# Moving a 4 MB memory-to-memory copy of a window state from the first projection to behind the samples' first seven page loads

## Chip, cores and metric

One core of one Trainium2 chip runs the whole program in one launch. The metric is device time in microseconds (us) of that core, the median of several executions. Lower is better.

## What is computed

The program is one inference step of a two-layer decoder. A prompt of 512 tokens and 8 samples of 8 new tokens each go through the same weights. Layer 0 mixes differential attention (4 heads) and sparse attention (4 query heads, with compressed, selected and window branches), layer 1 is gated linear attention, and each is followed by a squared-ReLU MLP (1024 to 4096 to 1024). Each sub-layer's input is scaled and shifted by a modulation computed from a conditioning vector (`silu(c) @ ada_w + ada_b`).

One of the fourteen outputs matters here. The window branch keeps, for every sample, the last 256 rows of keys and values. The new state drops the oldest 8 rows and appends the 8 new ones:

```python
win_all = jnp.concatenate([win_buf, jnp.stack([kw, vw], axis=2)], axis=1)   # win_buf: (8, 256, 2, 2, 128) f32
...
return y, (ka, va, cmp_new, sel_new, win_all[:, S:])                        # S = 8
```

So 248 of the 256 rows per sample are plain copies of an input: 8 x 248 x 512 x 4 bytes, 3968 KB, moved from device memory to device memory without passing through any engine's arithmetic. No computation of the step reads the copied output.

## The kernel before

The tensor engine (PE) carries the work, in this order: turning the inputs, the samples' compression (L980), the **first projection** (L1082 to L1084), the prompt's compression (L1131), the **prompt's attention** (`p_scores`, `p_turn`, `p_values`, L1168 to L1213), the **samples' attention** (`s_keys` to `s_back`, L1250 to L1301), the output projection, the MLP of layer 0, layer 1, and the second MLP. ScalarE (ACT) and VectorE (DVE) evacuate its results and split weights into high and low parts.

**The first projection** goes over 7 blocks of 512 columns (queries, keys, values, and so on, `pj_units`, L501), each over 5 tiles of tokens (four of 128 prompt tokens, one of the 64 sample tokens). A tile is 8 steps of three matmuls of 512 columns. Between the tiles PE does one unit of the modulation: `ada_late(0, u - 1)` (L946), which folds the last unit (L935), waits for the 1 MB of `ada_w` that this unit needs (L952), and multiplies it (L927, 32 small matmuls).

**SP's queue** is an order written out by hand (L649 to L789). For this stage it alternates `load_late(0, i)` (L686, 1 MB each into one of two places, waiting at L690 until PE has multiplied the unit before the last one) with `load_in(j)` (L712, two weights of 1 MB for a projection block). So a load of `ada_w` is requested when PE has ended a unit, and needed two units later.

**POOL's queue** (L791 to L899) loads 16 cached pages for the compression (L804), zeroes two scratch tiles (L809, L810), requests the copy of the state (L812), then stores each finished tile of keys and values (L834 to L849), and then requests the pages for the samples' attention, in a loop over 16 half steps `v` (L856). Even `v`: two pages of keys and two of values (L867); odd `v`: two pages of the selected branch (L871) and one load of the window state (L873). There are 8 places (`KV_PLACES`) in the weight ring for them. The place of `v == 7` holds something of the prompt's attention, so POOL waits there for its end (`o_kept`, L861). Later half steps wait until PE has used a place (L863). At the program's end POOL waits for everything that it sent, the copy included (L899).

Of the kernel before, what the change touches and what calls it, by code (L numbers as in the profile page):

```python
# [35 lines left out]
NS, DS = 8, 8  # L36
# [3 lines left out]
PAST, PAGE = 256, 128  # L40
# [76 lines left out]
def decoder_program(nc, a, out, const_cols):  # L117

    ctx = ExitStack()
    with ctx, nc.allow_non_contiguous_dma(reason="small vectors, gate columns"):  # L120
# [3 lines left out]
        def sem(name):  # L124
            return ctx.enter_context(nc.semaphore(name))
# [251 lines left out]
        out_stored = sem("out_stored")  # L377
# [415 lines left out]
        def _(pool):  # L793
# [15 lines left out]
            pool.memset(qAs[:, :, :, :], 0.0).then_inc(scratch_zero, 1)  # L809
            pool.memset(qBs[:, :, :, :], 0.0).then_inc(scratch_zero, 1)  # L810

            pool.dma_start(out[12][0][:, 0:PAST - DS], a["state_win_kv"][0][:, DS:PAST]).then_inc(out_stored, 16)  # L812

            def kv_out(o_p, o_s, t):

                if t < NT:
                    return o_p[t * P:(t + 1) * P]
                return o_s
# [37 lines left out]
            for v in range(2 * NS):  # L856
                n = v // 2
                if v == 4:
                    pool.wait_ge(cmp_mm, 3)
                if v == KV_PLACES - 1:  # L860
                    pool.wait_ge(o_kept, HA + HB)  # L861
                if v >= KV_PLACES:
                    pool.wait_ge(spv_mm, v - KV_PLACES + 1)  # L863
                if v % 2 == 0:
                    for b, cache in enumerate((ck, cv)):
                        for pg in range(NPAGE):
                            pool.dma_start(kvb[v % KV_PLACES][:, 2 * b + pg, :], cache[bass.ds(page[n * NPAGE + pg], 1)].rearrange("o t c -> (o t) c")  # L867
                                           ).then_inc(kv_loaded[v % KV_PLACES // 2], 16)
                else:
                    for pg in range(NPAGE):  # L870
                        pool.dma_start(kvb[v % KV_PLACES][:, pg, :], cs[bass.ds(page[n * NPAGE + pg], 1)].rearrange("o t c -> (o t) c")  # L871
                                       ).then_inc(kv_loaded[v % KV_PLACES // 2], 16)
                    pool.dma_start(kvb[v % KV_PLACES][:, 2:4, :], win[n]).then_inc(kv_loaded[v % KV_PLACES // 2], 16)  # L873
# [29 lines left out]
        def _(pe):  # L903
# [164 lines left out]
            def token_tile(banks, tiles, base, split=None, gate=False):  # L1068

                for k in range(KC):  # L1070
                    if split is not None:
                        pe.wait_ge(h_split, split + k + 2)
                    _, w_hi, w_lo = unit(base + k // 4, 4)
                    for bank, (u, t) in zip(banks, tiles):
                        x_hi, x_lo = h_high_x(k, t), h_low(k, t)
                        if gate:
                            at = ps[:, 7, 32 * t:32 * t + 24]
                            pe.matmul(at, x_hi, gwin_r[:, k, :], start=k == 0, stop=False)
                            mm = pe.matmul(at[:, 0:12], x_lo, gwin_r[:, k, 0:12], start=False, stop=k == KC - 1)
                            if t == NT and k == KC - 1:  # L1080
                                mm.then_inc(gate_mm, 1)
                        pe.matmul(bank, x_hi, w_hi[:, k % 4, :], start=k == 0, stop=False)  # L1082
                        pe.matmul(bank, x_hi, w_lo[:, k % 4, :], start=False, stop=False)  # L1083
                        mm = pe.matmul(bank, x_lo, w_hi[:, k % 4, :], start=False, stop=k == KC - 1)  # L1084
                        if k == KC - 1:
                            mm.then_inc(gin_mm if u is None else pj_mm, 1)
# [254 lines left out]
            def out_projection(layer):  # L1341
# [5 lines left out]
                def products(m, k, parts):  # L1347

                    _, w_hi, w_lo = unit(base + m // 2)
                    hi, lo = w_hi[:, k, m % 2 * P:(m % 2 + 1) * P], w_lo[:, k, m % 2 * P:(m % 2 + 1) * P]  # L1350
                    first, last = k == come[0], k == come[-1]
                    for i in parts:
                        bank = ps[:, 2 * (m % 4) + i, 0:HALF]
                        pe.matmul(bank, hi, h_hi[:, k, halves[i]], start=first, stop=False)  # L1354
                        pe.matmul(bank, hi, hT_r[:, k, halves[i]], start=False, stop=False)  # L1355
                    for i in parts:
                        mm = pe.matmul(ps[:, 2 * (m % 4) + i, 0:HALF], lo, h_hi[:, k, halves[i]], start=False, stop=last)  # L1357
                    if last:
                        mm.then_inc(out_mm, 1)
# [35 lines left out]
            def mlp(layer):  # L1395
# [4 lines left out]
                def half_products(g, k, half):  # L1400

                    _, w_hi, w_lo = unit(g // 2)
                    hi, lo = w_hi[:, k, g % 2 * P:(g % 2 + 1) * P], w_lo[:, k, g % 2 * P:(g % 2 + 1) * P]
                    bank, cols = ps[:, 2 * g + half, 0:HALF], halves[half]
                    pe.matmul(bank, hi, h_hi[:, k, cols], start=k == 0, stop=False)
                    pe.matmul(bank, hi, hT_r[:, k, cols], start=False, stop=False)
                    mm = pe.matmul(bank, lo, h_hi[:, k, cols], start=False, stop=k == KC - 1)
                    if half and k == KC - 1:
                        mm.then_inc(up_mm, 1)
# [1519 lines left out]
```

## Time and profile before

| what | value |
|---|---|
| median of 3 runs | 1866.79 us (1862.47 to 1869.63) |
| the profiled execution, own time | 1866.58 us |
| its span, first to last instruction | 1864.9 us |
| PE busy | 96% of the span |
| DVE, ACT, POOL busy | 46%, 25%, 4% |
| mean granted clock of PE | 0.954 of full speed |
| mean DMA rate | 117 GB/s |

The page of the profile shows 40 slices of the span, 46.6 us each. The first projection lies in slices 2 to 7, the prompt's attention in 7 to 10, the samples' in 10 and 11. A granted clock of 1.00 is 2.4 GHz and one of 0.50 is 1.2 GHz. The chain of waits is followed back from the last instruction: what stands in it was, one after the other, what the end waited for.

### The profile page before, as it was taken

How to read it: one execution, taken by the hardware profiler on the slowest of the kernel's cores; microseconds unless marked ns; L12 is line 12 of the kernel's file. 1: busy time of each engine (PE TensorE's matmuls, PEld its weight loads, DVE VectorE, ACT ScalarE, POOL GpSimd, SP SyncE). 2: the span in 40 equal slices, each digit the busy share in tenths (PEclk: the TensorE clock that was granted, in tenths of full speed). 3: DMA queues.
4: the chain of work that ended last, by engine and by line, in shares of the span. 5: the costliest groups of instructions: out<-in, count | busy, mean ns of one | idle time of the engine just before them, and what ended most of it. 6: DMA issues, size and time to landing. Idle time of an engine off the chain costs nothing.

```text
span 1864.9 us, 32781 instructions
## 1 busy us (share of the span) xinstructions
PE 1782.5 (96%) x14208; PEld 1628.2 (87%) x14208; DVE 861.4 (46%) x1653; ACT 472.8 (25%) x774; POOL 78.4 (4%) x146
## 2 busy tenths in 40 slices
PE   6989999899889999999999899999989999999998
PEld 5868888678759999999999897788889999999997
DVE  4543333444344664545353623344465836444542
ACT  3412121234463321111111323122323211111112
POOL 2000001400120000000000000000000000000000
PEclk8999999989899999999999999888779999999998
DMA  9876664500171323222223455222133222222211
GB/s 350 287 251 231 208 204 128 218 1 1 48 236 36 91 91 91 68 90 90 69 89 127 149 172 174 86 71 94 52 119 91 83 76 90 84 73 90 90 46 51
DMA packets 160191, 219.02 MB, mean 117 GB/s; under 512 B 7271, under 2 KB 131198, under 8 KB 159630
## 3 DMA queue, kind: packets, MB, share of 16 engines
q1 hardware_dynamic: 148814, 177.52, 29.4%
q0 software_dynamic: 11264, 39.86, 6.0%
q8 instruction: 88, 1.44, 0.3%
q14 instruction: 25, 0.20, 0.0%
HBM read 199.66 MB, written 21.76 MB: 119 GB/s over the span
## 4 chain that ended last, share of the span: by engine, by line
PE 89%; DVE 5%; DMA 2%; issue 2%; ACT 1%; POOLq 0%; POOL 0%; ACTq 0%; DVEq 0%
PE ps L1451 14%; PE ps L1449 14%; PE ps L1448 13%; PE ps L1082 4%; PE ps L1084 4%; PE ps L1083 4%; PE ps L927 2%; PE ps L1194 2%; PE ps L1354 2%; DMA arena<-in_ada_w 2%; PE ps L1355 2%; PE ps L1357 2%; PE ps L1180 2%; PE ps L980 2%; PE ps L1209 1%
## 5 line engine op out<-in xcount | busy, mean ns | idle before, releaser
L1448 PE MATMUL ps<-arena_r,wring_r 128*128 128x288 f32 x1920 | 532.8, 292 | 0.0
L1451 PE MATMUL ps<-arena_r,wring_r 128*128 128x288 f32 x1920 | 411.3, 295 | 0.0
L1448 PEld LDWEIGHTS ps<-arena_r,wring_r 128*128 128x128 f32 x1920 | 360.5, 188 | 0.0
L1451 PEld LDWEIGHTS ps<-arena_r,wring_r 128*128 128x128 f32 x1920 | 307.0, 188 | 0.0
L1449 PE MATMUL ps<-arena_r,wring_r 128*128 128x288 f32 x1024 | 284.5, 294 | 0.0
L1922 ACT ACTIVATE wring_r<-wring 128x2048 fp32r<-128x2048 f32 x64 | 122.4, 1916 | 576.5 <-DMA wring<-in_mlp_w 576.5
L1449 PE MATMUL ps<-hbuf_r,wring_r 128*128 128x288 f32 x896 | 249.0, 294 | 0.0
L1449 PEld LDWEIGHTS ps<-arena_r,wring_r 128*128 128x128 f32 x1024 | 192.4, 188 | 0.0
L2664 DVE SCALAR_TENSOR_TENSOR xbuf<-ps,mod,xbuf 128x288 f32<-128x288 f32 (+1 forms) x128 | 56.1, 480 | 245.4 <-PE ps L1451 245.4
L1449 PEld LDWEIGHTS ps<-hbuf_r,wring_r 128*128 128x128 f32 x896 | 168.3, 188 | 0.0
L2636 DVE TENSOR_TENSOR wring_r<-wring,wring_r 128x2048 fp32r<-128x2048 f32 x64 | 146.2, 2285 | 6.1 <-ACT wring_r L1922 5.0
L1082 PE MATMUL ps<-wring_r,xbuf_r 128*128 128x512 f32 x360 | 149.0, 414 | 0.0
L1083 PE MATMUL ps<-wring_r,xbuf_r 128*128 128x512 f32 x360 | 141.2, 392 | 0.0
L1084 PE MATMUL ps<-wring_r,hbuf_r 128*128 128x512 f32 x360 | 141.0, 392 | 0.0
L2650 DVE TENSOR_SCALAR arena<-ps 128x576 f32<-128x576 f32 x64 | 48.4, 756 | 131.2 <-PE ps L1451 131.2
L2193 DVE TENSOR_TENSOR wring_r<-wring,wring_r 128x2048 fp32r<-128x2048 f32 x34 | 77.6, 2290 | 36.3 <-ACT wring_r L1717 35.4
L1082 PEld LDWEIGHTS ps<-wring_r,xbuf_r 128*128 128x128 f32 x360 | 68.2, 189 | 19.1 <-issue 6.1
L1354 PE MATMUL ps<-arena_r,wring_r 128*128 128x288 f32 x256 | 76.9, 306 | 4.3 <-DVE hbuf_r L2303 3.0
L1084 PEld LDWEIGHTS ps<-wring_r,hbuf_r 128*128 128x128 f32 x360 | 68.0, 189 | 14.9
L1083 PEld LDWEIGHTS ps<-wring_r,xbuf_r 128*128 128x128 f32 x360 | 68.3, 190 | 11.4
L1355 PE MATMUL ps<-hbuf_r,wring_r 128*128 128x288 f32 x256 | 75.5, 300 | 0.0
L1357 PE MATMUL ps<-arena_r,wring_r 128*128 128x288 f32 x256 | 68.3, 298 | 0.0
(395 smaller groups left out, 2755.1 us busy)
## 6 DMA issues: line engine op xcount, KB each, us to landing
wring<-in_mlp_w SPq DMA_DIRECT2D x64, 1024.0 KB, 5.7
arena<-in_ada_w SPq DMA_DIRECT2D x40, 1024.0 KB, 6.1
wring<-in_even_w_in SPq DMA_DIRECT2D x14, 1024.0 KB, 7.4
wring<-in_gla_w_in SPq DMA_DIRECT2D x12, 1024.0 KB, 5.6
wring<-in_ada_w SPq DMA_DIRECT2D x4, 2048.0 KB, 18.2
xbuf<-xspill SPq DMA_DIRECT2D x2, 2304.0 KB, 9.4
arena<-in_cache_cmp_kv POOLq DMA_DIRECT2D x16, 256.0 KB, 6.8
wring<-in_cache_diff_k POOLq DMA_DIRECT2D x16, 256.0 KB, 3.8
```

Of the source, the lines that this page charges most:

```text
L1082: pe.matmul(bank, x_hi, w_hi[:, k % 4, :], start=k == 0, stop=False)
L1083: pe.matmul(bank, x_hi, w_lo[:, k % 4, :], start=False, stop=False)
L1084: mm = pe.matmul(bank, x_lo, w_hi[:, k % 4, :], start=False, stop=k == KC - 1)
L1354: pe.matmul(bank, hi, h_hi[:, k, halves[i]], start=first, stop=False)
L1355: pe.matmul(bank, hi, hT_r[:, k, halves[i]], start=False, stop=False)
L1357: mm = pe.matmul(ps[:, 2 * (m % 4) + i, 0:HALF], lo, h_hi[:, k, halves[i]], start=False, stop=last)
L1448: pe.matmul(bank, hi, x_hi[:, k, cols], start=k == 0, stop=False)
L1449: pe.matmul(bank, hi, x_lo[:, k, cols], start=False, stop=False)
L1451: mm = pe.matmul(bank, lo, x_hi[:, k, cols], start=False, stop=k == KC - 1)
L1922: act.activation(high, raw, ACT.Copy).then_inc(w_high, 1)
L2193: dve.tensor_tensor(low, raw, high.bitcast(F32), ALU.subtract).then_inc(w_split, 1)
L2636: dve.tensor_tensor(low, raw, high.bitcast(F32), ALU.subtract).then_inc(w_split, 1)
```

## The change

The request of the copy is taken from its place ahead of the loop over projection tiles, and put into the loop over the samples' half steps, at `v == 7`, before the wait for the end of the prompt's attention. Nothing else is different.

```diff
@@ -809,8 +809,6 @@
             pool.memset(qAs[:, :, :, :], 0.0).then_inc(scratch_zero, 1)
             pool.memset(qBs[:, :, :, :], 0.0).then_inc(scratch_zero, 1)
 
-            pool.dma_start(out[12][0][:, 0:PAST - DS], a["state_win_kv"][0][:, DS:PAST]).then_inc(out_stored, 16)
-
             def kv_out(o_p, o_s, t):
 
                 if t < NT:
@@ -858,6 +856,7 @@
                 if v == 4:
                     pool.wait_ge(cmp_mm, 3)
                 if v == KV_PLACES - 1:
+                    pool.dma_start(out[12][0][:, 0:PAST - DS], a["state_win_kv"][0][:, DS:PAST]).then_inc(out_stored, 16)
                     pool.wait_ge(o_kept, HA + HB)
                 if v >= KV_PLACES:
                     pool.wait_ge(spv_mm, v - KV_PLACES + 1)
```

## Rows read from the trace of the kernel before

**Rows 1.** Page: busy time, and shares of the chain of waits

```profile
PE 1782.5 (96%) x14208; PEld 1628.2 (87%) x14208; DVE 861.4 (46%) x1653; ACT 472.8 (25%) x774; POOL 78.4 (4%) x146
PE 89%; DVE 5%; DMA 2%; issue 2%; ACT 1%; POOLq 0%; POOL 0%; ACTq 0%; DVEq 0%
```

**Rows 2.** Waits of PE, 100 to 335 us: total, times, longest

```profile
PE ps L927 <- DMA arena<-in_ada_w: 7.2, 1, 7.2
```

**Rows 3.** Chain of waits, 88 to 135 us: start, length, what

```profile
101.97 20.54 DMA arena<-in_ada_w
122.51 0.04 issue
122.56 1.90 PE ps L927 x32
124.46 0.73 PE ps L1082
125.18 0.43 PE ps L1083
125.61 0.42 PE ps L1084
...
131.37 0.99 PE ps L927 x32
```

**Rows 4.** Chain of waits, 142 to 156 us, the same work undisturbed

```profile
145.97 0.99 PE ps L927 x32
146.96 0.43 PE ps L1082
147.39 0.23 PE ps L1083
147.62 0.23 PE ps L1084
...
153.21 0.99 PE ps L927 x32
```

**Rows 5.** Timeline of PE around the gap: start, length, instruction, idle before

```profile
115.09 0.29 PE L935 MATMUL ps<-cf,arena 128*128 128x18 f32 x2
122.56 1.90 PE L927 MATMUL ps<-arena,scT 128*9 128x128 f32 x32 [7.18 <-DMA arena<-in_ada_w]
```

**Rows 6.** Stretches: us, PE, PEld, DVE, ACT, POOL busy, granted clock, DMA share, GB/s

```profile
120.00:124.00 4.00, 1.44 (x28) 1.10 (x32) 0.00 (x0) 0.00 (x0) 0.00 (x0) 0.50 0.91 291
140.00:300.00 160.00, 160.00 (x1247) 131.49 (x1246) 59.09 (x140) 39.46 (x76) 13.04 (x24) 1.00 0.59 195
```

**Rows 7.** Timeline of POOL's queue

```profile
96.00 0.62 POOL L812 DMA_DIRECT2D out<-in_state_win_kv  x1
133.88 0.57 POOL L834 DMA_DIRECT2D out<-arena  x1 [37.26 <-DVE arena L2344]
...
344.72 1.11 POOL L867 DMA_DIRECT2D wring<-in_cache_diff_k  x2
...
357.51 1.06 POOL L867 DMA_DIRECT2D wring<-in_cache_diff_v  x2
489.42 1.06 POOL L871 DMA_DIRECT2D wring<-in_cache_sel_kv  x2 [130.84 <-DVE hbuf L2431]
```

**Rows 8.** DMA, 102 to 120 us: packets, MB, share of 16 engines; copy's time to landing

```profile
q0 software_dynamic: 56, 3.05, 39.8%
q1 hardware_dynamic: 1348, 1.36, 24.4%
out<-in_state_win_kv POOLq DMA_DIRECT2D x1, 3968.0 KB, 24.1
```

**Rows 9.** DMA issues at 94.7, at 109.2 and at 161.5 us: time to landing

```profile
arena<-in_ada_w SPq DMA_DIRECT2D x1, 1024.0 KB, 5.0
arena<-in_ada_w SPq DMA_DIRECT2D x1, 1024.0 KB, 16.3
arena<-in_ada_w SPq DMA_DIRECT2D x1, 1024.0 KB, 9.4
```

**Rows 10.** DMA, 383 to 488 us: all its queues

```profile
q8 instruction: 5, 0.08, 0.3%
q14 instruction: 4, 0.03, 0.1%
```

**Rows 11.** DMA, 358.6 to 383 us: its queues

```profile
q0 software_dynamic: 881, 2.90, 31.5%
q8 instruction: 2, 0.03, 0.5%
q14 instruction: 1, 0.01, 0.1%
```

**Rows 12.** Chain of waits, 540 to 552 us

```profile
547.93 2.17 issue
```

## Prediction, made before the changed kernel was run

> **What bounds the kernel now.** I read the page first: PE is busy 96% of the span and holds 89% of the chain that ended last, with DMA at 2% [rows 1]. A change of DMA order alone can win only where PE stands and waits for a transfer, so I asked for PE's waits in the projection. There is one, and only one: 7.2 us at the modulation's multiply L927, for its `ada_w` [rows 2]. The chain shows the same place: it leaves PE at 101.97 us, follows one transfer for 20.54 us, and comes back at 122.56 us [rows 3]. The timeline gives the gap itself as 7.18 us [rows 5].
>
> Why is that transfer late? POOL requests the state's copy at 96.00 us [rows 7], and it takes 24.1 us to land [rows 8], so it moves until 120.1 us. The 1 MB requested at 94.7 us, just ahead of it, landed in 5.0 us; the one at 101.97 us took 20.5 us and landed 2.4 us after the copy; the one at 109.2 us took 16.3 us [rows 3, 9]. Between 102 and 120 us the copy's queue carried 3.05 MB in 56 packets and 39.8% of the 16 engines' time, against 1.36 MB in 1348 packets for SP's queue [rows 8]. That is at most 0.398 x 16 x 18 / 56 = 2.0 us per packet of the copy on average, and 54 KB each: large pieces, behind which the 1 KB packets of a weight stand. Outside the copy the same order of loads keeps PE at 160.00 busy us of 160 [rows 6].
>
> **The change part by part.**
>
> *Taken away, the gap.* Without the copy the load requested at 101.97 us should land as its neighbours do: in 5.0 us with nothing beside it, in 9.4 us as the one at 161.5 us that queues behind two projection weights [rows 9]. PE wants it when L935 ends, 115.09 + 0.29 = 115.38 us [rows 5], which is 13.4 us after the request. At worst 4.0 us are left, so the whole 7.18 us go.
>
> *Taken away, the slow clock behind it.* After the gap the granted clock is 0.50, that is 1.2 GHz, in the stretch 120 to 124 us, and before it fell PE had been idle since 115.38 us [rows 5, 6]. The next instructions are slower than the same ones at 146 us: L927 1.90 against 0.99, L1082 0.73 against 0.43, L1083 0.43 and L1084 0.42 against 0.23 each [rows 3, 4]. That is 0.91 + 0.30 + 0.20 + 0.19 = 1.60 us. As a check, from one L927 to the next is 131.37 - 122.56 = 8.81 us there and 153.21 - 145.97 = 7.24 us undisturbed, 1.57 us apart. Together 7.18 + 1.60 = 8.8 us on the path.
>
> *What is late next.* The load of 109.2 us is then wanted at 115.38 + 7.24 = 122.6 us; with 9.4 us it is there at 118.6 us, 4.0 us early. The two weights requested near 114.8 us and the `ada_w` behind them are the pattern of 161.5 us, which has no gap [rows 6, 9]. I put 0 on it, and 1 us as its far end.
>
> *Put in, on POOL.* The request is one instruction of 0.62 us. At its old place POOL waited 37.26 us right behind it, so taking it out brings nothing there. At the new place it follows the 25 requests of `v` 0 to 6 (344.72 to 358.57 us) and stands ahead of a wait of 130.84 us [rows 7]. It passes 49 stores and those 25 loads on the queue; the first store is at 133.88 us, after the copy has landed, and the 25 loads now have it behind them and not beside them. Cost 0. Were the wait short, the cost would be 0.62 us, as the request at 489.42 us would come that much later.
>
> *Put in, on the DMA engines.* In this trace's time the copy starts behind the page loads, which keep the engines busy a little past 360 us, and with the 24.1 us of before it lands at about 358.6 + 24.1 = 383 us, 2 or 3 us more if it waits for the pages. From 383 to 488 us the engines carry 9 packets in all, of instructions [rows 10], and POOL's next request is at 489.42 us [rows 7]. So at least 100 us of silence cover it. All of this comes 8.8 us earlier in the new kernel. Without that cover it would cost up to its 24.1 us.
>
> *What still moves beside it there.* Instruction fetches: 3 between 358.6 and 383 us [rows 11]. The trace doesn't show one of them behind the copy with a wait. The bounds are from nothing, as none of the three stops the chain now, to the 2.17 us of "issue" in the chain at 547.93 us, when the samples' stage hands over to a stage of weight loads [rows 12]. A gain is excluded: the change puts a transfer beside them and takes none away. I take 0, nearer to the row of the same stage, and keep 2.2 us per fetch, some 4 us for two, for the range. The Trainium skill, "Runtime: NRT & Kernel Launch", section "Instruction fetch mechanics", says that the next block of 256 instructions is fetched while the present one runs and calls the cost "mostly hidden"; by it the sum stays as it is. No row here proves it for a fetch beside a memory-to-memory copy.
>
> **Sum.** -7.18 - 1.60 + 0 + 0 = -8.8 us. The profiled execution took 1866.58 us itself, 1.7 us more than its span and 0.2 us under the median of the runs, so it is typical: 1866.6 - 8.8 = **1857.8 us**.
>
> **The rivals.**
>
> *Part of the gain is given back (0.10).* One or two fetches of the prompt's attention come late, PE idles 2 to 4 us, and some of the work behind runs at half clock, as the 1.6 us behind the gap. Price 2.2 to 5 us, time 1860 to 1863 us. For it: that stage waits on ACT and DVE in short steps, so each delay of any of the three shows. Against it: the fetches are few.
>
> *Slower: a fetch waits for the whole copy (0.03).* If an engine empties one queue before it turns to another, a fetch is held for what is left of the copy, up to 24.1 us, in the prompt's attention at about 350 to 375 us of the new trace. With nothing to cover it PE loses 24.1 + 1.6 us, the sum becomes +16.9 and the time 1883 us. The point from which it decides is a hold of about 8.8 + what the block under way covers. For it: the load of 101.97 us landed only once the copy had ended [rows 3, 8]. Against it: a fetch has to start just behind the copy's start, and SP's queue did move 1348 packets beside it [rows 8]. The Trainium skill, "DMA: Bandwidth & Descriptors", section "Queues, rings and completion order", says that an engine "drains a whole packet", typically 9 to 17 descriptors, before it switches; if each engine's part of the copy counts as one such packet, this rival is what follows. The trace neither refutes nor confirms it: it doesn't tell which engine served which packet.
>
> *The gap stays (0.05).* The load is late for another reason, say the first blocks' weights and constants, and the copy only happened to lie beside it. Time 1866.6 us. For it: both loads of that neighbourhood land late, and the trace doesn't say which engine served which packet. Against it: their landings follow the copy's start and end.
>
> *More than the gap goes (0.04).* The later stages fall otherwise on the clock's steps, and the half-clock stretch of the prompt's attention gets shorter. Time about 1854 us. The three runs of one kernel are 7 us apart, and something like this must be behind that.
>
> **How the numbers follow.** The forecast, gap gone and nothing new, has 0.78: 1857.8 us, with 3 us either way for how the medians fall (the runs of before scatter from 4.3 us below to 2.8 us above their median). The range goes down to 1852, for that scatter on top of the fourth rival, and up to 1864, for the give-back with scatter. The unmoved and the slower case are left out. About 0.5%, or 9.3 us, is what a measurement of this kernel can tell from no change, and the forecast is 0.5 us short of it. So within the forecast a little under half, 0.36 of 0.78, lies over 0.5% faster, and with the fourth rival's 0.03 the chance of faster is 0.39. Slower by over 0.5% is 0.03 from the one rival. The rest, 0.58, is within 0.5%.
>
> **What the changed profile would show.** Right: no wait of PE at L927 on `ada_w` between 100 and 335 us; the load of 102 us landing in 5 to 7 us; a granted clock of 1.00 throughout the projection; its end and POOL's first page load 8 to 9 us earlier than 344.72; the copy requested near 350 us, landed before 380 us; the wait for the prompt's attention still above 120 us; and the prompt's attention as long as before. Wrong: a gap at L927 that stays or comes back a tile later, or new "issue" steps in the chain between 350 and 380 us, or a stretch from the first page load to the samples' first half step that is more than 2 us longer.

## The result and the profile after

The changed kernel has a median of **1857.51 us** (1852.27 to 1859.28, 8 runs), against 1868.47 us (1861.19 to 1871.26, 8 runs) of the kernel before, measured beside it. The ratio is 0.9946, with a 95% interval from 0.9932 to 0.9960: about 10 us less, just over the 0.5% that I had called the least that can be told. Two later sets of runs of the same changed kernel gave 0.9952 and 0.9958 (below), so the forecast 0.9953 lies among the three. One execution of one kernel below took 2480.8 us and one of the kernel before 4285.34 us; they are in a slow state and left out of the ratios, and of the medians given.

The page of the changed kernel: PE as busy as before, with DMA at 1% of the chain of waits and not 2% [rows 1].

```profile
span 1855.8 us, 32781 instructions
PE 1781.9 (96%) x14208; PEld 1626.4 (88%) x14208; DVE 861.8 (46%) x1653; ACT 472.8 (25%) x774; POOL 78.5 (4%) x146
PE 91%; DVE 4%; issue 2%; DMA 1%; ACT 1%; POOLq 0%; POOL 0%; ACTq 0%; DVEq 0%
```

PE's busy time fell by 0.6 us, the span by 9.1 us: nearly all that went was idle time. The chain of waits, 88 to 135 us, answers to [rows 3] and [rows 5] (lines after the change stand one lower, so L926 is the multiply that was L927):

```profile
107.14 0.99 PE ps L926 x32
...
114.37 0.99 PE ps L926 x32
115.36 0.43 PE ps L1081
115.80 0.23 PE ps L1082
...
121.61 0.99 PE ps L926 x32
...
128.98 0.99 PE ps L926 x32
```

Every multiply starts 7.2 to 7.4 us behind the last one and takes 0.99 us. No transfer stands between them. The DMA view of the request at about 101 us, and the stretches 116 to 120 and 120 to 124 us (columns as in [rows 6]), in the second of which the clock had been 0.50:

```profile
arena<-in_ada_w SPq DMA_DIRECT2D x1, 1024.0 KB, 5.2
```

```profile
116.00:120.00 4.00, 4.00 (x20) 3.28 (x19) 0.40 (x2) 0.00 (x0) 0.00 (x0) 1.00 1.04 393
120.00:124.00 4.00, 4.00 (x49) 3.31 (x48) 2.45 (x7) 0.88 (x2) 0.00 (x0) 1.00 1.09 360
```

The load lands in 5.2 us, not 20.54 us. POOL's timeline answers to [rows 7]:

```profile
334.93 1.11 POOL L866 DMA_DIRECT2D wring<-in_cache_diff_k  x2
...
348.81 0.63 POOL L859 DMA_DIRECT2D out<-in_state_win_kv  x1
480.20 1.09 POOL L870 DMA_DIRECT2D wring<-in_cache_sel_kv  x2 [130.77 <-DVE hbuf L2430]
```

The copy's request is now ahead of a wait of 130.77 us. It landed in 28.3 us, 4.2 us more than at its old place; the pages were still moving when it was requested. Nothing waited for it.

Where the 9.1 us between the two spans come from can be added up at marks that both traces have: the start of two `ada_w` multiplies (one ahead of the copy's request, one two units behind the gap), POOL's first page load, its request for half step 7, and the end:

| mark | before | after | difference | new in this part |
|---|---|---|---|---|
| a multiply L927 ahead of the copy | 93.68 | 92.68 | -1.00 | -1.00 |
| the multiply five units later | 138.75 | 128.98 | -9.77 | **-8.77** |
| first page load | 344.72 | 334.93 | -9.79 | -0.02 |
| request for half step 7 | 489.42 | 480.20 | -9.22 | +0.57 |
| end of the span | 1864.9 | 1855.8 | -9.1 | +0.1 |

The part in which the copy lay gives 8.77 us, against 8.8 us in the sum. This part is the one to measure by, since it hardly scatters. From the multiply ahead of the copy to the first page load it takes 251.04 us in the kernel before and 242.25 us in the changed one, and between 242.15 and 242.28 us in all seven traces whose copy isn't requested in the projection (after, e0, e10, e1, e3, e7, e9), whether there is no copy, one or four. The 8.8 us are thus shown against seven traces that agree to within 0.13 us; of the kernel before there is one trace. The 1.00 us ahead of it is older than the copy and can't be of its making: the other kernels below reach that mark anywhere from 92.5 to 94.4 us.

### The profile page after: what moved, and what is told of

The parts are those of the page before. It is cut to its first block, busy times and chain, and to the rows that moved or that the text cites. A ratio compares the mean times of both kernels' runs of the same rounds, so it can differ in the third digit from the quotient of the medians.

```text
span 1855.8 us, 32781 instructions
## 1 busy us (share of the span) xinstructions
PE 1781.9 (96%) x14208; PEld 1626.4 (88%) x14208; DVE 861.8 (46%) x1653; ACT 472.8 (25%) x774; POOL 78.5 (4%) x146
## 4 chain that ended last, share of the span: by engine, by line
PE 91%; DVE 4%; issue 2%; DMA 1%; ACT 1%; POOLq 0%; POOL 0%; ACTq 0%; DVEq 0%
PE ps L1450 14%; PE ps L1448 14%; PE ps L1447 13%; PE ps L1081 5%; PE ps L1083 4%; PE ps L1082 4%; PE ps L1193 2%; PE ps L926 2%; PE ps L1179 2%; PE ps L1353 2%; PE ps L1354 2%; PE ps L1356 2%; PE ps L979 2%; PE ps L1208 1%; PE ps L1583 1%
```

## The experiments

The theory to test was that the copy makes a load late that is wanted soon, and that at the new place nothing is wanted. Its rivals were that the gap belongs to that part of the projection whatever lies beside it, and that the copy costs something in the prompt's attention. Behind the first set a second question arose: is it the copy's bytes that hurt, the size of its pieces, or how many engines it holds?

**The changed kernel again** (e0, and e10 below), no edit.

> The changed kernel once more, as the measure for the runs sent with it. Theory (the gap at L927 was the copy's doing): 0.993 to 0.997 of the kernel before, about 9 to 11 us less, no wait of PE on ada_w in the projection. Rival (the gap only happened to lie there): a gap comes back in some execution.

Measured: 1858.27 us (9 runs), ratio 0.9952 (0.9938 to 0.9967), no wait on `ada_w`.

**No copy at all** (e1). This kernel leaves a part of one output unwritten (in the code shown here and below, ... stands for lines left out):

```diff
                 if v == KV_PLACES - 1:
-                    pool.dma_start(out[12][0][:, 0:PAST - DS], a["state_win_kv"][0][:, DS:PAST]).then_inc(out_stored, 16)
...
-            pool.wait_ge(out_stored, 16)
```

> Leaves the copy of the 248 old rows out altogether, so that part of one output is not written. Theory (at its new place the copy costs nothing): within 1.5 us of the changed kernel run beside it. Rival (the copy slows the prompt's attention at its new place, by late instruction fetches or through the clock): 2 to 5 us faster than the changed kernel, and the stretch from the first page load of the samples to the request of half step 7 shorter than the 145.3 us that the changed kernel takes.

Measured: 1857.08 us (8 runs), ratio 0.9951 (0.9933 to 0.9968), 1.2 us from e0, within the scatter. The stretch from the first page load to half step 7 is 480.68 - 334.66 = 146.0 us, a little longer than the 145.3 us with the copy. So at its new place the copy costs nothing that can be measured, and the changed kernel has all that this copy's order can give, to within the some 3 us that the interval of each ratio allows.

**Four copies at the new place** (e3; the lines that make the spare memory and wait for all four at the end are not shown):

```diff
                     pool.dma_start(out[12][0][:, 0:PAST - DS], a["state_win_kv"][0][:, DS:PAST]).then_inc(out_stored, 16)
+                    for i in range(3):
+                        pool.dma_start(spare[i], a["state_win_kv"][0][:, DS:PAST]).then_inc(out_stored, 16)
```

> At the new place four copies one behind another, three of them into spare device memory that nothing reads. Theory (the stage behind has nothing to do with the DMA engines): the copies take some 85 to 100 us, end before half step 7 at about 480 us, and the time stays within 1.5 us of the changed kernel. Rival (instruction fetches wait behind pieces): four times as many fetches beside copies, the prompt's attention 2 to 10 us longer, with issue gaps of 1 us and more in the chain between 360 and 450 us. Rival (a fetch waits for the whole queue): tens of us slower.

Measured: 1853.62 us (6 runs, 1850.95 to 1858.29), ratio 0.9935 (0.9918 to 0.9951), which overlaps the other two. The prompt's attention was not longer: 480.43 - 335.77 = 144.7 us, with 8 and 5 packets of instruction fetches in the 140 us around it. DMA view of this kernel, 330 to 470 us:

```profile
DMA  9199999989999999999991000000000000000000
q0 software_dynamic: 3280, 23.73, 49.3%
q8 instruction: 8, 0.13, 0.4%
q14 instruction: 5, 0.04, 0.1%
spare<-in_state_win_kv POOLq DMA_DIRECT2D x3, 3968.0 KB, 54.9
```

The engines are busy until about 407 us and PE doesn't notice. The rival of the whole queue falls: it wanted tens of us. The other, with 2 to 10 us more, finds nothing either, but its test is weaker than I had meant: the copies had 5 packets of fetches beside them (349 to 407 us) against 3 beside the one copy, not four times as many. One thing I had wrong: I expected 85 to 100 us for four copies one behind another. They landed in pairs, the first two 31.3 and 31.6 us after their requests, the other two 54.9 and 56.5 us. Two copies thus took little longer than one, and the next two moved behind them.

**The copy at its old place in 2 KB rows** (e2), the order of rows turned so that the pieces can't be merged:

```diff
-            pool.dma_start(out[12][0][:, 0:PAST - DS], a["state_win_kv"][0][:, DS:PAST]).then_inc(out_stored, 16)
+            pool.dma_start(out[12][0][:, 0:PAST - DS].rearrange("n t v g d -> t n (v g d)"), a["state_win_kv"][0][:, DS:PAST].rearrange("n t v g d -> t n (v g d)")).then_inc(out_stored, 16)
```

> The copy stays at its old place, but its order of rows is turned, so that it goes in pieces of 2 KB and not of 62 KB. Theory A (weights stand behind large pieces, one or more per engine): engines now alternate fairly, the load of 102 us lands in 8 to 12 us, before PE wants it 13.4 us after its request; no gap; time within 2 us of the changed kernel. Theory B (the bytes themselves are too many, 4 MB ahead of 1 MB): the load still lands after the copy, the gap is 5 to 9 us, the time that of the kernel before.

Measured: 1865.23 us (12 runs), ratio 0.9992 (0.9980 to 1.0005). PE's waits and DMA, 94 to 126 us:

```profile
PE ps L927 <- DMA arena<-in_ada_w: 4.2, 1, 4.2
```

```profile
DMA  0799993765579987555579997557799975879999
q0 software_dynamic: 2000, 4.07, 34.5%
out<-in_state_win_kv POOLq DMA_DIRECT2D x1, 3968.0 KB, 28.5
```

The load took 17.5 us, so theory A of this run fell: small pieces alone do little. The gap is 3 us shorter, but the half clock behind it lasts longer, until about 124 us, so that only 2 us of time come back. Theory B had the time right and the rest wrong: the gap of 4.2 us is under its 5 us, and the load landed at 118.6 us, 5 us ahead of the copy (95.1 + 28.5 = 123.6 us) and not behind it. The queues' packets between 106.8 and 110 us, with the load still outstanding:

```profile
q0 software_dynamic: 130, 0.53, 40.8%
q1 hardware_dynamic: 129, 0.13, 11.6%
```

One packet of the load (1 KB) moved for each packet of the copy (2 KB). In the kernel before, between 108 and 110 us, it was one for each packet of 62 KB, and the load stood all but still:

```profile
q0 software_dynamic: 7, 0.44, 52.9%
q1 hardware_dynamic: 8, 0.01, 1.2%
```

The slices of e2 show something that neither theory had: in the stretches where the copy is alone, and in the one just shown, the engines' busy share is about 0.5 at about 200 GB/s. I read that as half of the 16 engines at work, in 2 KB rows as in large pieces (the records don't name the engine, only the share). The four copies together had 0.9 and more, and their landing in pairs fits: two of them fill the engines. That made the next two runs.

**The copy at its old place over all engines, 31 KB pieces** (e4), one request per sample:

```diff
-            pool.dma_start(out[12][0][:, 0:PAST - DS], a["state_win_kv"][0][:, DS:PAST]).then_inc(out_stored, 16)
+            def rows_flat(x):
+                return x.rearrange("t v g d -> (t v g d)").rearrange("(a b) -> a b", a=16)
+
+            for n in range(NS):
+                pool.dma_start(rows_flat(out[12][0][n, 0:PAST - DS]), rows_flat(a["state_win_kv"][0][n, DS:PAST])).then_inc(out_stored, 16)
...
-            pool.wait_ge(out_stored, 16)
+            pool.wait_ge(out_stored, 16 * NS)
```

> The copy at its old place as 8 requests, one per sample, each cut into 16 pieces of 31 KB, one for each of the 16 engines (the one request of before keeps about half of the engines busy: DMA share 0.5 while it is alone). Theory A (what hurts is that half of the engines are held for 20 us): the copy now takes 11 to 14 us, ends near 110 us, the load of 101 us lands before PE wants it at 114.4 us or up to 2 us late; time 0 to 3 us above the changed kernel. Theory B (a copy from memory to memory can't go faster than about 200 GB/s, however it is spread): it still lands 24 us or more after its request, gap of 5 us and more, the time of the kernel before.

Measured: 1859.42 us (6 runs), ratio 0.9957 (0.9943 to 0.9972); the load landed in 14.0 us, the gap was 0.7 us. Both fit theory A.

**The same over all engines in 1 KB rows** (e5), one request:

```diff
-            pool.dma_start(out[12][0][:, 0:PAST - DS], a["state_win_kv"][0][:, DS:PAST]).then_inc(out_stored, 16)
+            pool.dma_start(out[12][0][:, 0:PAST - DS].rearrange("n t v g d -> (t v) n (g d)"), a["state_win_kv"][0][:, DS:PAST].rearrange("n t v g d -> (t v) n (g d)")).then_inc(out_stored, 16)
```

> The copy at its old place as one request in 3968 pieces of 1 KB, spread over 16 engines. Theory A (engines held): lands in 14 to 20 us, as small pieces cost more each; a gap of 0 to 3 us, time between the changed kernel and the one with 2 KB rows (1858 to 1864 us). Theory B (bytes through memory): as the 2 KB rows, a gap of 4 us, 1865 us.

Measured: 1857.27 us (6 runs), ratio 0.9951 (0.9937 to 0.9965). The copy landed in 18.0 us, the load in 14.3 us, and PE waited 0.9 us. PE's waits (60 to 325 us) and DMA (94 to 126 us) of this kernel:

```profile
PE ps L927 <- DMA arena<-in_ada_w: 0.9, 1, 0.9
```

```profile
DMA  0006899989999999999998999999999999999999
out<-in_state_win_kv POOLq DMA_DIRECT2D x1, 3968.0 KB, 18.0
```

The copy's 4.06 MB stand in 1008 packets in this trace, so four rows of 1 KB go in one. With the copy at its very old place, but its share of the engines doubled, the kernel's median is that of the changed one. The steadier measure, from the multiply ahead of the copy to the first page load, is 1.0 us longer than in the changed kernel (243.22 against 242.25 us), 0.7 us in e4 and 7.0 us in e2. The reading that fits all of these runs is that half of the engines were held for some 20 us, and that a load has a part on each of them and has landed only when its last part has. Small pieces alone took 3 us off the gap, the spread took 6 us off it, with large pieces as with small ones. Spreading also shortens the copy itself, and no run tells the two apart: the same work on twice the engines is over sooner.

**The copy in the middle of the projection** (e6), the request as it was:

```diff
-            pool.dma_start(out[12][0][:, 0:PAST - DS], a["state_win_kv"][0][:, DS:PAST]).then_inc(out_stored, 16)
...
                 elif j == VA:
+                    if t == 1:
+                        pool.dma_start(out[12][0][:, 0:PAST - DS], a["state_win_kv"][0][:, DS:PAST]).then_inc(out_stored, 16)
                     pool.dma_start(kv_out(*dv, t), va[0:M, t, :]).then_inc(v_stored, 16)
```

> The copy as it was, but requested at the second tile of values, about 165 us, in the middle of the projection. Theory (the gap goes with the copy): no gap at 115 us, but one of 6 to 13 us at a multiply L927 between 178 and 195 us, with half clock behind it; time 8 to 14 us above the changed kernel, so that of the kernel before or a little slower. Rival (the early projection is special, as its first weights and constants load there): no gap anywhere, time of the changed kernel.

Measured: 1872.93 us (12 runs), ratio 1.0032 (1.0020 to 1.0044): 15 us above the changed kernel. PE's wait, and the chain around it:

```profile
PE ps L928 <- DMA arena<-in_ada_w: 14.4, 1, 14.4
```

```profile
166.80 26.89 DMA arena<-in_ada_w
193.69 0.04 issue
193.74 1.90 PE ps L928 x25
195.63 0.73 PE ps L1083
```

The gap went with the copy; it and the time are a little over the upper ends that I gave (13 us and 14 us). It is twice as long; this load was requested 0.8 us behind the copy and not 6 us. The rival that the early projection is special falls. The traced execution is the slowest of the twelve (1878.42 us), so its gap can be longer than the usual one.

This trace also shows what the loads lacked. The queues between 183 and 189 us, with two loads outstanding, and SP's queue between 191 and 194 us, when the copy had landed (at 189.4 us):

```profile
q0 software_dynamic: 35, 1.06, 46.7%
q1 hardware_dynamic: 39, 0.04, 1.9%
```

```profile
q1 hardware_dynamic: 542, 0.55, 51.3%
```

Half of the engines' time was free in the first stretch, and yet the loads hardly moved, 39 packets of 1 KB in 6 us. In the second they were alone and still had only half of the time, at 192 GB/s, against a share of 1.04 and 393 GB/s in the row of 116 to 120 us above. The plain reading is that what was left of the loads stood behind the copy on half of the engines, and that the other half had done its part.

**The same place over all engines in 1 KB rows** (e8), the edit of e5 at the place of e6.

> The copy at the second tile of values, as in the run that had a gap of 14.4 us there, but as one request in 3968 pieces of 1 KB over 16 engines. Theory (it is the holding of half of the engines that makes a load late, not the copy's bytes or its place): the copy lands in 16 to 20 us, the gap shrinks to 0 to 4 us, time 0 to 5 us above the changed kernel (1857 to 1863 us). Rival (the bytes count; the early place was lucky, since its load had been requested 5 us behind the copy and not right behind it): a gap of 8 us and more, 1868 us and more.

Measured: 1864.98 us (11 runs), ratio 0.9988 (0.9977 to 0.9998). The wait shrank from 14.4 to 3.6 us, as expected, but the time is 1864.98 us, 2 us above the upper end that I gave. The load took 16.1 us here (its request at 173.8 us is the one after that of e6). So the spread takes most of the gap away and not all: 4 MB ahead of 1 MB take their time on 16 engines too. Not all of the gain is the spread's. POOL takes 2.04 us over this request and 0.62 us over the old one, and the load requested 0.8 us behind it, which was the late one of e6, landed in 5.2 us, ahead of the copy's bytes. Like against like are the next loads: 22.8 us in e6, 16.1 us here.

**The copy behind the last page load** (e7):

```diff
-            pool.dma_start(out[12][0][:, 0:PAST - DS], a["state_win_kv"][0][:, DS:PAST]).then_inc(out_stored, 16)
...
+            pool.dma_start(out[12][0][:, 0:PAST - DS], a["state_win_kv"][0][:, DS:PAST]).then_inc(out_stored, 16)
             pool.wait_ge(gin_mm, V_HALF)
```

> The copy requested behind the samples' last page load, about 523 us, ahead of the wait for layer 1. There the output projection's four weights follow on SP's queue, from 527 us. Theory (what counts is whether a load that is wanted within 20 us shares the engines with the copy): these weights land up to 20 us late, PE waits at the start of the output projection, time 5 to 15 us above the changed kernel. Rival (weights are requested early enough there, or behind the copy's start only in part): within 2 us of the changed kernel.

Measured: 1873.30 us (11 runs), ratio 1.0029 (1.0014 to 1.0044), 15 us above the changed kernel. An output projection weight takes 5.4 us to land in the median of the changed kernel. Here the chain of waits, 520 to 565 us, reads:

```profile
529.04 22.23 DMA wring<-in_even_w_out
551.28 0.02 issue
551.30 0.02 ACT wring_r L1717
...
553.12 1.07 ACT arena L1872 x2
554.19 0.05 issue
554.24 0.24 PE ps L1268
```

What waits is not the output projection, as I had expected. ACT has the rounding of this weight (L1717) in its order ahead of the last exponentials of the samples' attention (L1872), so PE waited 15.2 us at L1268 in the samples' attention. Behind the last page load is as bad a place as the middle of the projection.

**The same over all engines** (e9), the edit of e5 at the place of e7.

> The copy behind the last page load, as in the run whose output projection waited 15.2 us, but in 3968 pieces of 1 KB over 16 engines. Theory (half of the engines held): the first two weights land 8 to 12 us after their request and not 20 or more, the wait shrinks to 3 to 8 us, as the weights were wanted almost at once; time 1861 to 1866 us. Rival (the bytes count): the wait of 15 us stays, 1873 us.

Measured: 1866.24 us (12 runs), ratio 0.9990 (0.9975 to 1.0005), wait 9.9 us. The time is 0.2 us above the upper end of the theory, and the wait 2 us above it: the weight came 16.9 us after its request, not 8 to 12 us. Half of the loss goes with the spread (15.0 to 7.1 us above the changed kernel beside it), in e8 three fifths (14.7 to 5.8 us). Here too the traced execution is the slowest of its twelve, 1870.68 us.

**The changed kernel a third time** (e10).

> The changed kernel once more beside these two, as their measure: 0.993 to 0.997 of the kernel before.

Measured: 1859.18 us (8 runs), ratio 0.9958 (0.9941 to 0.9975).

## Why the prediction was right

*The gap.* Expected 7.18 us, all of it gone. It is gone, and e6 shows that the gap follows the copy while e1 shows that it is gone without one. The margin of "at worst 4.0 us" was in truth 8 us: the load took 5.2 us.

*The slow clock.* Expected 1.60 us. Gap and slow clock together are the change between the first two marks, 8.77 us against 8.8 us. The granted clock of 116 to 124 us is 1.00. In e6, where the gap was 14.4 us, the next multiply follows the one behind the gap after 9.4 us (193.74 to 203.16) and not 6.8 us (203.16 to 209.95), so 2.6 us of half clock there.

*What is late next.* Expected nothing. PE is busy 160.00 of 160 us from 140 to 300 us, as before [rows 6].

*POOL.* Expected nothing. The request sits ahead of 130.77 us of waiting.

*Engines and fetches at the new place.* Expected 0, with up to 4 us kept. e1 and e3 bound it: with no copy and with four the prompt's attention is equally long, to within what it scatters by itself. In the nine traces without a copy there it takes 145.7 us in the mean (141.7 to 148.2), in the four with one or more 146.6 us (144.7 to 149.6). A cost of 1 us can't be told from none. The rule of the Trainium skill, "Runtime: NRT & Kernel Launch", section "Instruction fetch mechanics", that an instruction fetch is mostly hidden fits these copies, with at most 5 packets of fetches beside them. My sign of being wrong, more than 2 us longer in this stretch, was too narrow: the changed kernel is 0.6 us longer there than the kernel before in its first trace and 4.9 us in e10, and the program is the same. Whether an engine empties a whole packet of one queue before it turns to the next (the Trainium skill, "DMA: Bandwidth & Descriptors", section "Queues, rings and completion order") can be told in part: between the copy's queue and SP's queue the counts were 130 to 129 packets in e2 and 7 to 8 in the kernel before, as turns of one packet each would give. For a fetch it stays open, as the records don't name the engine. What fell is the consequence that I drew for fetches.

*The explanation was right in its place and only half of the cause.* I put the late load down to "large pieces, behind which the 1 KB packets of a weight stand". The size does set how far a load gets beside the copy: it landed 2.4 us behind a copy of large pieces and 5 us ahead of one of 2 KB rows. But e2 shows that this takes only 3 us off the gap, e4 and e5 that spreading takes off 6 us, with pieces of 31 KB as with 1 KB. The number of engines held is what my reading of the DMA share of 39.8% had in it [rows 8], and I didn't take it out.

*The size.* 1857.8 us was said, 1857.51 us measured. That agreement is in part luck: the kernel before measured 1868.47 us and not the 1866.6 us that I started from, and the difference was 11 us and not 8.8 us, and the two cancel. The measured difference of the first set is 11 us of medians, those of the other two sets 8.8 us (e0) and 7.7 us (e10). The working's 8.8 us is what the projection gives back, which the marks confirm to within 0.1 us; the rest is scatter of the stages behind it. Over 0.5% or within it was close to a coin's toss, as the chances said: one set came out over it, two within. The first page load came 9.79 us earlier and not 8 to 9, for the 1.00 us that is older than the copy.

## What to carry to other kernels

A bulk copy that nobody reads should be requested where no load follows within its own duration, which the DMA rates of the stages show, and not merely late in the program: behind the last page load it cost 15 us. If there is no such stage, shape it so that the engines' busy share is near 1 while it moves; one whose share is 0.5 while it is alone held half of the engines here, by the reading of e2 to e6, and each load that had a part there waited for it. Price a gap with the half-clock instructions behind it, and not in proportion. The part up to the first page load was longer than in the changed kernel by 0.7 us for a wait of 0.7 us (e4), 1.0 for 0.9 (e5), 5.2 for 3.6 (e8), 7.0 for 4.2 (e2), 8.8 for 7.2 (before) and 17.1 for 14.4 (e6). Behind the two shortest waits the granted clock stayed at 1.00.

## What was not expected of the hardware

The prompt's attention scatters more than anything that the change did there. From the first page load to half step 7 it took 144.7 us (kernel before), 145.3 us (after), 144.7 us (four copies), 146.0 us (no copy), 482.24 - 335.52 = 146.7 us (e0) and 485.19 - 335.64 = 149.6 us (e10). The shortest is 479.30 - 337.60 = 141.7 us (e5), which has no copy there either. The changed kernel, e0 and e10 are the very same program and lie 4.3 us apart; the kernel with no copy lies among them, and the one with four copies at the kernel before. The granted clock of that stretch tells them apart (e0, e10 and the four copies; columns as in [rows 6], so the clock is the third number from the end):

```profile
336.00:482.00 146.00, 141.56 (x924) 108.63 (x923) 70.44 (x225) 58.66 (x183) 14.09 (x26) 0.93 0.21 79
```

```profile
336.00:485.00 149.00, 144.69 (x924) 110.82 (x923) 70.53 (x225) 58.76 (x183) 14.16 (x26) 0.91 0.20 78
```

```profile
336.00:480.00 144.00, 139.90 (x923) 107.06 (x915) 70.19 (x224) 58.76 (x183) 16.01 (x29) 0.94 0.48 165
```

The same 924 matmuls take 141.56 us at a clock of 0.93 and 144.69 us at 0.91. PE works there in short steps between waits for DVE and ACT, and which of them fall into a half-clock stretch differs from one execution to the next: from 336 to 360 us the mean clock is 0.72 in the changed kernel's trace and in e0, and 0.59 in e10. That is some 5 us of the 7 to 10 us by which runs of one kernel differ; what decides it was not tested.

Copies from device memory to device memory can move as fast as loads do: the four of e3 moved, at first beside the pages, at some 290 to 400 GB/s, while one alone in its old shape stays near 200 GB/s.
